# Opening of a fused transformer kernel: first modulation group split in two, eight weight buffers instead of four

## The reference, cut to what matters here

```python
mod_l = split(silu(c) @ w_mod + b_mod, 6)          # w_mod is 2048 x 12288
mod_c = split(silu(c_ctx) @ w_mod + b_mod, 6)
hl = rms_norm(x, norm1_g) * (1 + mod_l[1]) + mod_l[0]
zl = hl @ w_in + b_in                              # w_in is 2048 x 13312
a1, a2 = zl[:, :1024], zl[:, 1024:2048]
u = a1 * sigmoid(a2)                               # then a convolution of 31 taps
```

## Time and profile before

| | |
|---|---|
| median of 3 runs | 3055.17 us (3052.7 to 3057.91) |
| the profiled execution's own time | 3050.99 us |
| its span in the trace | 3049.2 us |
| PE busy in the span | 3003.7 us (99%) |
| DVE busy | 2127.2 us (70%) |
| mean DMA rate | 184 GB/s |
| first product of the opening starts | 49.87 us |
| last product of the opening ends | 189.57 us |

### The profile page before, as it was taken

How to read it: one execution, slowest core, us unless ns; L and a number is a source line. 1 busy time by engine, 2 the same in 40 slices (tenths; PEclk the granted TensorE clock), 3 DMA queues, 4 the chain that set the end, 5 groups by cost and what they waited for, 6 DMA issues and landing times.

```text
span 3049.2 us, 52430 instructions
## 1 busy us (share of the span) xinstructions
PE 3003.7 (99%) x22975; PEld 2780.9 (91%) x22975; DVE 2127.2 (70%) x3212; ACT 333.2 (11%) x659; POOL 71.9 (2%) x137
## 2 busy tenths in 40 slices
PE   6999999999999999999999999999999999999998
PEld 3688847999999999999999999999999998899998
DVE  1039976468868877766778877867667576995765
ACT  1021010122220000111010000001012102000010
POOL 0000000110000000000000000000000000000000
PEclk9999999999999999999999999999999999999999
DMA  8998554554457855655777555565444654543443
GB/s 294 308 308 275 180 185 154 158 163 138 136 170 259 294 166 170 187 167 166 249 249 248 166 166 166 167 180 178 141 139 139 209 178 125 152 139 111 125 152 111
DMA packets 578352, 561.55 MB, mean 184 GB/s; under 512 B 24573, under 2 KB 548432, under 8 KB 570701
## 3 DMA queue, kind: packets, MB, share of 16 engines
q1 hardware_dynamic: 546272, 466.65, 49.7%
q0 software_dynamic: 13856, 80.90, 7.3%
q10 hardware_dynamic: 17997, 10.67, 1.2%
HBM read 549.66 MB, written 8.51 MB: 183 GB/s over the span
## 4 chain that ended last, share of the span: by engine, by line
PE 90%; DVE 6%; DMA 3%; issue 0%; ACT 0%; SPq 0%; DVEq 0%; ACTq 0%; POOLq 0%
PE psum L497 40%; PE psum L477 17%; PE psum L670 3%; DVE arena L2049 3%; PE psum L573 2%; PE psum L566 2%; PE psum L608 2%; PE psum L919 2%; PE psum L933 2%; PE psum L924 2%; PE psum L932 2%; PE psum L547 2%; PE psum L927 2%; PE psum L922 2%; PE psum L934 2%; PE psum L537 1%
## 5 line engine op out<-in xcount | busy, mean ns | idle before, releaser
L497 PE MATMUL psum<-arena 128*128 128x128 f32 x6400 | 732.1, 275 | 0.8 <-DVE arena L1837 0.8
L497 PEld LDWEIGHTS psum<-arena 128*128 128x128 f32 x6400 | 723.3, 192 | 7.9 <-issue 6.2
L477 PE MATMUL psum<-arena,ring 128*128 128x256 f32 (+2 forms) x2944 | 700.7, 398 | 0.6 <-ACTq L1224 0.6
L477 PEld LDWEIGHTS psum<-arena,ring 128*128 128x128 f32 x2944 | 555.6, 190 | 131.1 <-issue 62.7
L497 PE MATMUL psum<-arena,ring 128*128 128x128 f32 x4416 | 508.3, 275 | 0.0
L497 PEld LDWEIGHTS psum<-arena,ring 128*128 128x128 f32 x4416 | 500.8, 192 | 0.7 <-DVE arena L1871 0.4
L1823 DVE TENSOR_TENSOR arena<-ring 128x2048 f32<-128x2048 f32 x104 | 238.4, 2292 | 242.2 <-PE psum L497 213.9
L1802 DVE TENSOR_TENSOR arena<-ring,arena 128x1024 f32<-128x1024 f32 (+1 forms) x192 | 188.1, 980 | 6.0
L1802 DVE TENSOR_TENSOR arena<-arena 128x512 f32<-128x512 f32 (+6 forms) x269 | 143.6, 534 | 16.4 <-DVE arena L2818 5.7
L1837 DVE TENSOR_TENSOR arena<-ring,arena 128x1024 f32<-128x1024 f32 x104 | 127.4, 1225 | 3.6
L2667 DVE TENSOR_TENSOR arena<-ring 128x1024 f32<-128x1024 f32 x64 | 78.4, 1225 | 69.5 <-PE psum L919 68.7
(11 more groups left out here) (360 smaller groups left out, 3329.0 us busy)
## 6 DMA issues: line engine op xcount, KB each, us to landing
ring<-w_ff SPq DMA_DIRECT2D x128, 1024.0 KB, 6.5
ring<-w_in SPq DMA_DIRECT2D x88, 1024.0 KB, 7.7
ring<-ab_w_in SPq DMA_DIRECT2D x56, 1024.0 KB, 6.3
arena<-w_mod POOLq DMA_DIRECT2D x48, 1024.0 KB, 7.1
ring<-cd_w_in SPq DMA_DIRECT2D x48, 1024.0 KB, 5.8
ring<-w_mod SPq DMA_DIRECT2D x32, 1024.0 KB, 6.9
ring<-w_in SPq DMA_DIRECT2D x32, 512.0 KB, 4.7
ring<-w_o SPq DMA_DIRECT2D x16, 1024.0 KB, 5.8
```

The source lines that it names most:

```text
L477: mm = pe.matmul(psum[:, s, m * N:(m + 1) * N], w[:, k, m * P:(m + 1) * P], x(k)[:, 0:N], start=(j == 0), stop=(j == kt - 1))
L497: return pe.matmul(o, z, w, **kw) if tokens else pe.matmul(o, w, z, **kw)
```

## The change

- Group 0 of 512 columns becomes two groups of 256: `GROUPS` lists (first tile, tiles) as (0,2), (2,2), (4,4), (8,4), (12,4). A mod load of a small group holds 8 row tiles of 256 columns, still 1 MB, so a small group has four mod loads, and `lead` issues 8 float32 products of 256 columns for each (16 instructions).
- Product loads are wide: for the small groups one load of four banks and one of three, for the large groups two banks, two, two and one. 28 product loads become 16; the opening has 48 loads. Their bytes are the same.
- Every second set of four loads goes to `EXTRA`, four buffers in parts of `arena` that are free at the time, under four borrowed semaphores. A load waits for the release of the load eight before it, not four.
- The tokens are turned after q = 1 and q = 3; the spread root, the packs and the columns of group 0 follow after q = 3. DVE copies the packs after it has normed the tokens, no longer before. Taps are turned after q = 7.
- ACT issues the first two packs ahead of the silu.
- The first two chunks are released two loads later in the list (`CHUNK_AT` -2 and -1 in place of -4 and -3). The counts of the borrowed semaphores move with it.

```diff
-OPENING = [("mod", 0, s, k) for s in range(2) for k in range(4)]
-for _g in range(3):
-    _mod = [("mod", _g + 1, s, k) for s in range(2) for k in range(4)]
-    for _i in range(7):
-        _n = 2 if _i == 0 else 1
-        OPENING += _mod[:_n] + [("product", _g, _i, 0)]
-        _mod = _mod[_n:]
-OPENING += [("product", 3, i, 0) for i in range(7)]
+GROUPS = ((0, 2), (2, 2), (4, 4), (8, 4), (12, 4))
+HALF_SLOTS = ((0, 4), (4, 3))
+OPEN_SLOTS = ((0, 2), (2, 2), (4, 2), (6, 1))
+OPENING = [("mod", 0, s, k) for s in range(2) for k in range(2)]
+for _g in range(5):
+    _slots = HALF_SLOTS if _g < 2 else OPEN_SLOTS
+    _mod = [("mod", _g + 1, s, k) for s in range(2) for k in range(GROUPS[_g + 1][1])] if _g < 4 else []
+    _each = len(_mod) // len(_slots)
+    for _n, (_i, _w) in enumerate(_slots):
+        OPENING += _mod[_each * _n:_each * _n + _each] + [("product", _g, _i, _w)]
...
-CHUNK_AT = (-4, -3, 0, 1, 2, 3, *(3 + g for g in CHUNK_PARTS), 25, 25, 26, 27, 28, 29, 30, 31, 32, 33, 34, 35, 36, 36,
+CHUNK_AT = (-2, -1, 0, 1, 2, 3, *(3 + g for g in CHUNK_PARTS), 25, 25, 26, 27, 28, 29, 30, 31, 32, 33, 34, 35, 36, 36,
...
+        EXTRA = [at(o, 2048) for o in (12288, 31984, 36080, 38128)]
+        EXTRA_LOAD = ["load_s5", "load_s5b", "load_s5c", "load_glw"]
...
+        def in_ring(j):
+
+            return (len(OPENING) - 1 - j) // 4 % 2 == 0
+
...
+            def opening_load(j, src, width, size):
+
+                s = j % 4
+                if j >= 8:
+                    sp.wait_ge(sem(f"slot{s}_used"), (j - 8) // 4 + 1 + (s == 3))
+                buffer = ring[:, s, :] if in_ring(j) else EXTRA[s]
+                sp.dma_start(buffer[:, 0:size].rearrange("p (k n) -> p k n", n=width), src).then_inc(
+                    sem(f"load_slot{s}" if in_ring(j) else EXTRA_LOAD[s]), 16)
...
-                for k in range(4):
-                    mm = pe.matmul(psum[32 * k:32 * k + 32, 7, :], cvec[:, 4 * quad + k, :], w[:, k, :],
-                                   start=(quad == 0), stop=(quad == 3))
+                for k in range(rows):
+                    r = 32 * (k % 4)
+                    mm = pe.matmul(psum[r:r + 32, 7, 0:tiles * P], cvec[:, rows * part + k, :], w[:, k, :],
+                                   start=part == 0 and k < 4, stop=part == tiles - 1 and k >= rows - 4)
...
-                if q == 5:
+                if q == 1:
                     pe.wait_ge(sem("load_x"), n["load_x"].next())
                     for t in range(0, HT, 2):
                         turn_tokens(XN, t, t // 2, "act")
-                elif q == 6:
+                elif q == 3:
+                    for t in range(HT, KT, 2):
+                        turn_tokens(XN, t, t // 2 - 4, "act")
+                    pe.wait_ge(sem("token_diagonal"), n["token_diagonal"].next())
+                    take(4, "dve")
...
                     n["load_packs"].n = sum(len(p) for p in PACKS)
                     pe.wait_ge(sem("load_packs"), n["load_packs"].now())
                     for j in range(5):
                         r = sum(r for _, r in PACKS[j])
                         turn([(PACK[j][0:r, :], 0)], 4 + j % 2, "dve")
...
+                    pe.wait_ge(sem("pick_ready"), n["pick_ready"].next())
+                    lead_columns(0, 6)
```

More of the change, by code:

```diff
@@ L653, in lead_columns, with open_product @@
                 mm.then_inc(sem(full("dve", b)), n[full("dve", b)].up())
[L655 to L675, removed]
+            def open_product(q):
+                _, g, first, wide = OPENING[q]
+                t0, tiles = GROUPS[g]
+                w = opening_slot(q, 256 * wide, tiles)
+                for b in range(first, first + wide):
+                    c = "act" if b < 4 else "dve"
+                    if g == 0:
+                        take(b, c)
+                        pe.matmul(psum[:, b, :], OPENZERO[:, 0:P], OPENZERO[:, :], start=True, stop=False)
+                    for k in range(tiles):
+                        if b == 0:
+                            pe.wait_ge(sem("input_tile"), n["input_tile"].next())
+                        if b == 6 and k == tiles // 2 and g < 4:
+                            lead_columns(g + 1)
+                        for m in range(2):
+                            o = 256 * (b - first) + m * P
+                            mm = pe.matmul(psum[:, b, m * T:(m + 1) * T], w[:, k, o:o + P], HL[:, t0 + k, :],
+                                           start=False, stop=g == 4 and k == tiles - 1 and m == 1)
+                            if b == first and k == m == 0:
+                                leave(mm, q % 4)
+                    if g == 4:
+                        mm.then_inc(sem(full(c, b)), n[full(c, b)].up())
@@ L1249, in _, with load_packs @@
             load(XN, dram["x"].rearrange("(t p) n -> p t n", p=P), "load_x")
+            def load_packs(order):
+                for j in order:
+                    r0 = 0
+                    for name, rows in PACKS[j]:
+                        load(PACK[j][r0:r0 + rows, :], dram[name].rearrange("(r p) -> r p", p=P), "load_packs")
+                        r0 += rows
+            load_packs((1, 0))
             act.wait_ge(sem("cvec_zero"), n["cvec_zero"].next())
@@ L1256, in _ @@
             act.sem_inc(sem("cvec_ready"), n["cvec_ready"].up())
[L1257 to L1262, removed]
+            load_packs((3, 2, 4))
             load(TAPN[0:TAPS, :], dram["conv_w"], "load_taps")
@@ L1785, in _ @@
                 sem("norm_var"), n["norm_var"].up())
[L1787 to L1793, removed]
             def step(ins):
@@ L1927, in lead_columns @@
                 v.wait_ge(sem(free("dve", b)), n[free("dve", b)].now())
-                step(v.scalar_tensor_tensor(out=gain[:, 0:2, k], in0=mod[:, KT + 4 * g:KT + 4 * g + 4, :].rearrange(
-                    "p k q -> p q k"), scalar=1.0, in1=over(col("norm1_g", 4 * g, 4), 2), op0=ALU.add, op1=ALU.mult))
+                step(v.scalar_tensor_tensor(out=gain[:, 0:2, k], in0=mod[:, KT + t0:KT + t0 + tiles, :].rearrange(
+                    "p k q -> p q k"), scalar=1.0, in1=over(col("norm1_g", t0, tiles), 2), op0=ALU.add, op1=ALU.mult))
                 done()
-                for k in range(4 * g, 4 * g + 4):
+                for k in range(t0, t0 + tiles):
                     v.tensor_scalar(HL[:, k, :], HL[:, k, :], gain[:, 0, k:k + 1], mod[:, k, 0:1], ALU.mult,
@@ L1949, in _ @@
             v.sem_inc(sem("x_normed"), n["x_normed"].up())
+            for j in range(5):
+                b = 4 + j % 2
+                v.wait_ge(sem(full("dve", b)), n[full("dve", b)].next())
+                rows = sum(r for _, r in PACKS[j])
+                v.tensor_copy(cols[:, j * P:j * P + rows], psum[:, b, 0:rows]).then_inc(
+                    sem(free("dve", b)), n[free("dve", b)].up())
+                v.wait_ge(sem(free("dve", b)), n[free("dve", b)].now())
             lead_columns(0)
```

93 lines of the change are left out of this document (52 added, 41 removed).

## The result

The changed kernel takes 3031.41 us in the median of four runs (3030.83 to 3031.87), the kernel before 3053.93 (3049.76 to 3057.91): ratio 0.9929, interval 0.9913 to 0.9945. Run again beside other kernels it took 3032.89 against 3051.63, ratio 0.9940 (0.9927 to 0.9954).

A forecast was written before the change was run, and what follows sets the result against it. PE mostly waits until the first product, then bounds the opening. Start 35.0, work 138.5 and leftover 3.7 put the opening's end at 177.2 us, 12.4 earlier: 3055.17 - 12.4 = 3042.8 us, whole range 3036 to 3049.

The forecast's parts named there:

- Start of the products: Head of the opening, through tokens, norm, packs and columns: PE starts on load 4 at 35.0 us, bounds 34.4 to 37.
- I take 1.9: Mods of 256 columns in the small groups: 1.9 us each, priced at 0.12 us a pair of weight load and matmul.
- E: End of the last opening product: 189.57 us before the change, forecast at 177.2, 12.4 earlier.
- For the new opening I put 3.7: Leftover of the opening's products: 1.9 us for a slow start, 0.8 for zeroing, 1.0 for waits.
- Columns and taps: Column and taps work within the opening's groups: four tiles of columns at 1.88 us, taps and half columns 0.94 each.
- Behind the opening: Convolution and query products after the opening: everything moves by the same 12.4 us, nothing later depends on a fixed time.
- From span to median: Whole kernel: the 12.4 us gain read from the profiled span was subtracted unchanged from the median of 3055.17 us.
- first L670 at about 39 us: Sign to look for at the first opening product: it starts at about 39 us, after two mods at 1.9.
- that of cheap mods: Rival on the small groups: narrow mods cost 1.0 us and waits go too, gain 16 us, 3039; chance 0.11.
- The waits of before: Rival on the opening's transfers: leftover stays 9.8 us in place of 3.7, gain 6.3, 3049; chance 0.14.
- x wasn't late: Rival at the opening's head: x lands behind eight megabytes of weights, 15.7 us later, 3058 us; chance 0.05.
- half clock through the small groups: Rival on groups 0 and 1: products run at 1.2 GHz, kernel slower at 3065 us; chance 0.04.

The follow-up runs named there:

- the cut-in-two run: The changed kernel with each mod matmul cut into two of half the columns: 3033.14 us, ratio 0.9937 to the kernel before.

## Why the prediction was off

The direction and both mechanisms were right (earlier products, waits gone); the size was not. Point by point:

- **Start of the products: forecast 35.0 for load 4, measured 36.33.** The pole was named rightly: tokens, norm, packs, columns. ACT's squares began at 18.2 and not 16.4. The second lead started only at 15.21, where 14.04 had been taken over, and was done at 17.1; and ACT was issuing small transfers until 17.9. At the columns 1.0 us of that was left (34.54 for 33.5). The eight column matmuls took 1.8 in place of 0.94: the granted clock was 0.50, that is 1.2 GHz, from 34 to 36.3 us, behind the 5.66 us in which PE stood waiting for the packs. With the half microsecond that had been put for hops, it cost 1.3 us of gain.
- **The step "I take 1.9" for a narrow mod failed.** The two behind the first product load took 1.0 each, and two at a granted clock of 0.56 3.2 together. Two wide mods in a row take 1.85, four 3.57, not 2.0 and 4.0. The 28 mods from there to E take 5.2 + 8 x 1.85 + 2 x 3.57 = 27.2, where 31.6 was put: 4.4 us. The reason given for 1.9, that the count of pairs sets the price, is what the cut-in-two run refutes for mods.
- **The step "For the new opening I put 3.7" failed too**, a term mis-sized. Zeroing is there and took 1.5 (0.22 for each of seven banks). The 1.0 for waits and the 1.9 for a slow first product didn't come: PE waited for no transfer, and the granted clock was 1.00 from 39.5 us on, after PE had been busy without a gap from 34.5. That is 2.2 us less. In the second trace of the changed kernel the first product is a little slow (2.15 us for 1.89), so this term varies by some tenths from run to run.
- **Columns and taps** were put at 7.6 and took 6.5 (four tiles of columns 1.70 in steady state, 75.52 to 77.22, not the 1.88 of the first ones): 1.1 us less. The products took 0.2 less than their price.
- **Behind the opening: forecast 0, measured 1.3.** 0.8 of it lies ahead of the query products: from E to their start PE stood 0.44 us before, and nothing now, its wait of 0.51 for DVE's sums at 337.09 being gone. The other 0.5 was not followed.
- **From span to median: forecast 0, measured 2.3 in the first comparison** and nothing of the kind in the later ones. The reference run was one execution of a kernel whose runs differ by up to 10 us.

From 36.33 to 170.67 are 134.3 us, 7.9 less than 138.5 + 3.7, and 4.4 + 2.2 + 1.1 + 0.2 are these 7.9. In sum 12.4 - 1.3 + 7.9 - 0.1 (rounding) = 18.9 at E, + 1.3 behind it = 20.2. The sign "first L670 at about 39 us" came true by luck: the start was 1.3 later and the two mods 0.6 cheaper than put.

The prediction took PE to be at 1.2 GHz from 14 to 33 us, and its rows to agree with the page that it names. That rests on durations alone: mods of 1.94 against 1.0 at 102 us. The granted clock of that stretch reads 1.00. In the changed kernel it reads 1.00 too until 28 us, while the mods at 10.35 and 15.21 take 1.94 and those at 19.71 and 22.31 take 1.07. The durations show two speeds there that the column doesn't; why is open.

Of the rivals, that of cheap mods was right about them and would have been nearest (3039). Chunk 1 was used 8.96 us behind E (179.63), as forecast, and cost nothing. The waits of before didn't stay, x wasn't late (its transposes start at 17.1), and half clock through the small groups didn't come; with four buffers the granted clock falls to 0.77 from 60 to 90 us, which cost 5.6 us there and not 22. What the forecast didn't see is how much the two parts need each other: with four buffers the new order gains nothing at all.

What stays open: why the kernel before scatters more than its version with eight buffers is only argued (each wait and each slow stretch can fall otherwise); no second trace of it was taken. Some 1 us of the 23 of four buffers is neither in the listed waits nor in slow matmuls.

## What to carry to other kernels

Price an instruction by a row with the same operand shapes on both sides: 0.12 us of a pair with 128-column weights said nothing about pairs with 32-column weights, which take at most a quarter or so of it (33 ns). When transfers run near their top rate, count waits together with the slow clock that follows them, and test a change of order and a change of buffers in both combinations: here one alone gave 0 and 9 us, both 19 to 23. When two things end at nearly the same time, an edit to either looks worthless until the other is made too.

## What the runs showed of the hardware

- An issue on SP's queue isn't always short. In the changed kernel the issues of loads 4 to 6, at 11.3, 15.5 and 18.8 us, took 4.1, 3.3 and 8.3 us, and those at 48.1 and 49.7 us 0.37. What decides it isn't shown: with the taps' transfer split, the one of 8.3 took 4.0.
- With one small transfer of 31 rows on ACT's queue (124 KB) two weight loads on SP's queue took 17.9 us to land in the median; with the same transfer issued as 30 rows and one row they took 13.2.
- 32 pairs of weight load (32 columns) and matmul (128 columns of float32, in four strips of the array) run at 33 ns a pair: 1.05 us for the 32.
- The profile's granted clock can read 1.00 where matmuls run at half their speed: up to 28 us of the changed kernel, where the same mod took 1.94 and then 1.07.
